# Routing lists of 128 slots instead of 96, and the scatter's list moved from VectorE to ScalarE, in an encoder block with 64 experts

## What is computed

```python
def moe_ffn(x, router_w, router_bias, w_gate, w_up, w_down, sh_gate, sh_up, sh_down):
    scores = sigmoid(xf @ router_w); sel = scores + router_bias
    ...                                   # 4 of 8 groups, then the best 8 of 64 experts
    def expert_block(args):
        tok, e = args
        xb = x_pad[tok]
        hb = jax.nn.silu(xb @ w_gate[e]) * (xb @ w_up[e])
        return hb @ w_down[e]
    ...                                   # each row weighted, then summed into its token
    routed = jax.ops.segment_sum(yb, row_tok, num_segments=n_tok + 1)[:n_tok]
```

## Time and profile before

| | us |
|---|---|
| median of 3 runs (lowest, highest) | 1180.86 (1178.73, 1181.45) |
| the profiled execution | 1178.36 |
| its span | 1176.6 |
| PE busy | 1117.5 (95%) |
| DVE busy | 846.3 (72%) |
| ACT busy | 682.7 (58%) |
| POOL busy | 310.5 (26%) |

### The profile page before, as it was taken

One profiled execution on the slowest core, in us unless ns is written; L12 is line 12 of the kernel. 1 busy time (PEld: TensorE's weight loads), 2 busy tenths in 40 slices (PEclk: granted clock), 3 DMA queues, 4 the chain that ended last, 5 costly groups with the idle time before them and its releaser, 6 DMA issues.

```text
span 1176.6 us, 15711 instructions
## 1 busy us (share of the span) xinstructions
PE 1117.5 (95%) x5390; PEld 840.3 (71%) x5390; DVE 846.3 (72%) x1034; ACT 682.7 (58%) x689; POOL 310.5 (26%) x179
## 2 busy tenths in 40 slices
PE   4999999999999889999999999999999999999796
PEld 3878777768878566777777776777777777676475
DVE  6544436452445586999999988988989988887376
ACT  3332224451223324888888877877878877777354
POOL 1000000000002532444444433432434434231421
PEclk9999999998999899999999999999999999999899
DMA  8522313013345356999999999999999999998721
GB/s 312 179 72 72 99 45 108 1 36 143 108 144 195 138 186 233 346 365 374 369 373 368 369 359 364 366 369 360 353 361 367 368 365 354 364 360 263 257 101 54
DMA packets 68475, 294.78 MB, mean 251 GB/s; under 512 B 11216, under 2 KB 14288, under 8 KB 43600
## 3 DMA queue, kind: packets, MB, share of 16 engines
q1 hardware_dynamic: 52944, 256.43, 57.7%
q0 software_dynamic: 14912, 35.68, 12.3%
q10 hardware_dynamic: 576, 2.10, 0.4%
HBM read 275.29 MB, written 35.65 MB: 264 GB/s over the span
## 4 chain that ended last, share of the span: by engine, by line
PE 36%; DMA 17%; DVE 6%; ACT 3%; issue 3%; ACTq 0%; DVEq 0%; SPq 0%
DMA gu_raw<-in_moe_w_up 11%; PE ps L400 10%; PE ps L402 10%; PE ps L401 9%; DMA gu_raw<-in_moe_w_gate 5%; DVE w_lo L1674 3%; ACT w_hi L1566 3%; PE ps L1475 3%; PE ps L1929 1%; PE ps L1215 1%; PE ps L1499 1%; DVE w_lo L384 1%; PE ps L1466 1%; DVE grp L1283 0%; PE ps L1910 0%
## 5 line engine op out<-in xcount | busy, mean ns | idle before, releaser
L1674 DVE TENSOR_TENSOR w_lo<-gu_raw,w_hi 128x2048 fp32r<-128x2048 f32 x126 | 288.6, 2291 | 52.0 <-ACT w_hi L1566 50.7
L1566 ACT ACTIVATE w_hi<-gu_raw 128x2048 fp32r<-128x2048 f32 x128 | 242.3, 1913 | 53.0 <-DMA gu_raw<-in_moe_w_up 40.7
L400 PE MATMUL ps<-w_hi,xgT_hi 128*96 128x512 f32 x512 | 205.9, 402 | 5.9 <-issue 3.4
L402 PE MATMUL ps<-w_hi,xgT_lo 128*96 128x512 f32 x512 | 203.0, 397 | 0.0
L1777 POOL DMA_INDIRECT xg<-h_rows,get_idx x64 | 149.2, 2331 | 203.5 <-DVE get_idx L1662 171.8
L401 PE MATMUL ps<-w_lo,xgT_hi 128*96 128x512 f32 x512 | 201.6, 394 | 0.0
L400 PE MATMUL ps<-w_hi,act_hi 128*128 128x512 f32 x384 | 155.9, 406 | 5.9 <-PEq L496 2.8
L402 PE MATMUL ps<-w_hi,act_lo 128*128 128x512 f32 x384 | 151.3, 394 | 0.0
L401 PE MATMUL ps<-w_lo,act_hi 128*128 128x512 f32 x384 | 151.1, 393 | 0.0
L1679 DVE TENSOR_TENSOR dn_lo<-dn_raw,dn_hi 128x2048 fp32r<-128x2048 f32 x64 | 146.1, 2282 | 5.7 <-ACT dn_hi L1572 5.3
L1572 ACT ACTIVATE dn_hi<-dn_raw 128x2048 fp32r<-128x2048 f32 x64 | 122.2, 1910 | 12.6 <-issue 8.5
(11 more groups left out here) (203 smaller groups left out, 1722.5 us busy)
## 6 DMA issues: line engine op xcount, KB each, us to landing
gu_raw<-in_moe_w_gate SPq DMA_DIRECT2D x64, 1024.0 KB
gu_raw<-in_moe_w_up SPq DMA_DIRECT2D x64, 1024.0 KB
dn_raw<-in_moe_w_down SPq DMA_DIRECT2D x64, 1024.0 KB
raw<-in_w_in SPq DMA_DIRECT2D x18, 1024.0 KB, 5.1
h_rows<-x_rows SPq DMA_DIRECT2D x8, 512.0 KB, 5.0
raw<-in_w_out SPq DMA_DIRECT2D x4, 1024.0 KB, 5.6
ple_raw<-in_ple_w_gate SPq DMA_DIRECT2D x4, 1024.0 KB, 9.8
x_rows<-in_x SPq DMA_DIRECT2D x4, 512.0 KB, 10.3
```

The lines of the kernel that those rows point to most:

```text
L400: nc.tensor.matmul(out, x_hi, w_hi, start=first, stop=False)
L402: return nc.tensor.matmul(out, x_lo, w_hi, start=False, stop=last)
L1566: nc.scalar.activation(m.w_hi[:, 2 * x.b + half], m.gu_raw[:, 2 * x.b + half], ACT.Copy).then_inc(gu_hi, 1)
L1674: nc.vector.tensor_tensor(m.w_lo[:, 2 * x.b + half], m.gu_raw[:, 2 * x.b + half], m.w_hi[:, 2 * x.b + half].bitcast(F32), ALU.subtract).th ...
```

## The change

The list length goes from 96 to 128. The constant `slots` gets another arrangement: written in bits, partition p = 64h + 32u + 4g + v (h and u one bit, g three, v two) holds slot 32v + 16u + 8h + g. `put_idx` gets four buffers. `put_list(x)` leaves DVE; ACT now does it as the last thing of its step, after `scale_y(x-1)`, with an Identity and a bias from a new constant `far`, and waits for the scatter of x-4 where DVE waited for that of x-2. Two tiles move in memory.

```diff
-SLOTS = 96
+SLOTS = 128
...
-        self.put_idx = [at(f"put_idx{i}", [P, 1], U32, 180.75 + i * 0.0625) for i in range(2)]
+        self.put_idx = [at(f"put_idx{i}", [P, 1], U32, 180.75 + i * 0.0625) for i in range(4)]
...
-        self.hT_lo = at("hT_lo", [P, 2, 2 * cap], F32R, 181)
+        self.hT_lo = at("hT_lo", [P, 2, 2 * cap], F32R, 110)
-        self.onehot = at("onehot", [P, 2, NT, cap], BF16, 182.5)
+        self.onehot = at("onehot", [P, 2, NT, cap], BF16, 181)
...
-    nc.gpsimd.iota(m.slots[:, 0:rounds * cap].rearrange("p (r q j) -> p r q j", r=rounds, q=QUEUES),
-                   pattern=[[cap, rounds], [1, QUEUES], [QUEUES, cap // QUEUES]], base=0, channel_multiplier=0,
-                   allow_small_or_imprecise_dtypes=True)
+    parts = m.slots[:, 0:rounds * cap].rearrange("p (r h u g v) -> p r h u g v", r=rounds, h=2, u=2, g=8)
+    for u in range(2):
+        nc.gpsimd.iota(parts[:, :, :, u], pattern=[[cap, rounds], [8, 2], [1, 8], [32, 4]], base=16 * u,
+                       channel_multiplier=0, allow_small_or_imprecise_dtypes=True)
...
+            def put_list(x, at=99):
+
+                if at not in (0, 2):
+                    act.wait_ge(put[x.b], 16 * (x.turn2 - 2 + ZEROS[x.b]))
+                act.wait_ge(found, x.it + 1 + LEAD)
+                nc.scalar.activation(m.put_idx[x.q][0:CAP],
+                                     m.found[0:CAP, bass.ds(x.e, 1), 0:1].rearrange("p o c -> p (o c)"),
+                                     ACT.Identity, bias=m.far[0:CAP]).then_inc(put_ready, 1)
...
                     if at != 0:
                         scale_y(x.next(-1))
+                    put_list(x, at if first else 99)
...
-            def put_list(x):
-                dve.wait_ge(put[x.b], 16 * (x.turn2 - 1 + ZEROS[x.b]))
-                nc.vector.tensor_scalar(m.put_idx[x.b][0:CAP],
-                                        m.found[0:CAP, bass.ds(x.e, 1), 0:1].rearrange("p o c -> p (o c)"),
-                                        FAR, None, ALU.add).then_inc(put_ready, 1)
...
-                                             out_offset=bass.IndirectOffsetOnAxis(ap=m.put_idx[x.b][0:CAP], axis=0),
+                                             out_offset=bass.IndirectOffsetOnAxis(ap=m.put_idx[x.q][0:CAP], axis=0),
```

More of the change, by code:

```diff
@@ L32 @@
 ROUTED_SCALE = 2.5
-SLOTS = 96
+SLOTS = 128
 FAR = 4096.0
-QUEUES = 16
 HC = 2048
@@ L105, in __init__ @@
         self.peak_i = at("peak_i", [P, 1], I32, 206)
+        self.far = at("far", [P, 1], F32, 206.25)
         self.sh_down = at("sh_down", [P, HC], F32, 0)
@@ L164, in set_constants @@
     nc.gpsimd.memset(m.eps[:], LN_EPS).then_inc(base_set, 1)
-    pool.wait_ge(base_set, 7)
+    nc.gpsimd.memset(m.far[:], FAR).then_inc(base_set, 1)
+    pool.wait_ge(base_set, 8)
     for eye in (m.ident, m.ident_bf):
@@ L765, in _ @@
         def _(act):
-            act.wait_ge(base_set, 7)
+            act.wait_ge(base_set, 8)
             nc.scalar.activation(m.peak[:], m.eps[:], ACT.Sqrt)
@@ L1725, in step @@
                     split_down(x)
-                    if at != -1:
-                        put_list(x)
                 all_experts(dve, r, step)
                 split_hT(Expert(r, QUADS - 1, 3))
-                put_list(Expert(r, QUADS - 1, 3))
             dve.sem_inc(found, LEAD)
```

## The result

| | us |
|---|---|
| before, median of 9 runs (lowest, highest) | 1181.84 (1178.73, 1186.15) |
| after, median of 9 runs (lowest, highest) | 1176.16 (1173.85, 1178.32) |
| ratio, 95% interval | 0.9949, 0.9931 to 0.9967 |
| profiled execution, before and after | 1178.36, 1175.55 |
| its span, before and after | 1176.6, 1173.8 |

The changed kernel is 0.5% faster. The forecast was 1183.0, a little slower. The time that came out is that of rival A, 1176.9, and of rival D, 1177; which of the two mechanisms it was, the profile and the experiments have to tell.

A forecast was written before the change was run, and what follows sets the result against it. Transfers were taken to hold late experts (10.20 us each), a loop over PE, ACT and DVE the early ones. Early loss 0.8, start 0.5 and small packets 0.9 gave +2.2 us on 1178.36, carried to the median 1183.0; range 1172 to 1193.

The forecast's parts named there:

- rival A: Experts' transfers: lists over all 128 partitions make gathers and scatters cheaper, 9.0 us an expert; 1176.9 us; chance 0.22.
- rival D: Experts: faster products and shorter DVE queue count, additions lie in idle time; 4.5 us faster, 1177; chance 0.10.
- What bounds the kernel before: Experts: transfers set the late pace, 10.20 us each; early a loop of 9.70, measured 9.77, with transfers close behind.
- The loop: PE, ACT and DVE passing two experts: 19.39 us, plus 0.67 added, less 0.15, gives 19.91, 9.96 an expert.
- the transfers: Experts: same rows and weights moved, so late ones stay at 10.20 us; early ones lose 4.4, 3.6 given back.
- the forecast case: Whole kernel: the prediction's own outcome, 1183.0 us, from 1179 to 1187 by its bounds; chance 0.45.
- rows 12: Profile window read as a gather: 0.33 us a row, weights beside it at 25.6 GB/s an engine.
- signs put down for A: Experts: a gathered row at 0.16 us, or a DMA share clearly below 1.0, would show rival A.
- What the change removes: DVE between dn_lo and hT_lo: one 96x1 instruction and its wait go, worth nothing; four lists free nobody else.
- Small packets: Transfers: places without a row add 4096 packets of 9 ns, 2.3 us of the 16 engines, 0.9 counted.
- Rival B: Experts' transfers: the new arrangement loads the 16 engines unevenly; 11 us slower, 1194; chance 0.12.
- Rival C: Experts: the loop is longer than summed, 10.35 us instead of 9.96; 1191 taken; chance 0.11.

The follow-up runs named there:

- e1: Kernel before with only the scatter's list moved to ACT, last in the step, four buffers, lists still 96: 1178.83 us, ratio 0.9993.
- e5: e1 with all its transfers but 12 of 24 gate_up products and lighter work on ACT and DVE, lists of 96: 1175.38 us, ratio 0.9957 to before.
- e11: e10's code with lists of 96 in the arrangement of before: 1178.64 us, ratio 0.9998 to before.
- e6: Changed kernel with all its transfers and the same light work as e5, lists of 128: 1131.76 us, ratio 0.9592 to before.
- e7: e5 with every place of the scatter's lists out of range, so scatters move no rows: 1089.82 us, ratio 0.9232 to before.
- e9: e2 with four buffers for the scatter's list instead of two, list still on DVE: 1171.69 us, ratio 0.9937 to before.
- e2: Kernel before with lists of 128 in the new arrangement, scatter's list still on DVE with two buffers: 1192.28 us, ratio 1.0094.
- e3: Changed kernel with the old arrangement of slots (partition 8q + j holds slot 16j + q): 1242.6 us, ratio 1.0516 to before.
- e12: e6 with the old arrangement of slots (partition 8q + j holds slot 16j + q): 1227.14 us, ratio 1.0394 to before.
- e4: Changed kernel with the scatter's list made on ACT ahead of silu instead of behind the scaling of rows: 1173.49 us, ratio 0.9922 to before.
- e10: e4 with the gather's list moved to ACT too, lists of 128: 1160.8 us, ratio 0.9838 to before.

## Why the prediction was wrong

**What bounds the kernel before** was read rightly. Early experts 9.77 and late 10.20, the loop close below: e1, e5 and e11 confirm that with lists of 96 the transfers hold the pace (10.05, 10.11, 10.01 us), whatever is taken off the loop.

**The loop** was summed rightly. Predicted were 19.91 us for two experts; 19.95 were measured in one step. (The lower bound, given as 9.87 for one expert, is 9.84 by its own terms: 19.39 + 0.43 - 0.15, halved.) Its terms, from the groups of the whole span after (mean ns behind the busy us):

```profile
L1690 DVE TENSOR_TENSOR xgT_lo<-ps,xgT_hi 128x1024 fp32r<-128x1024 f32 x64 | 77.9, 1218 | 3.9 <-ACT xgT_hi L1578 3.9
...
L1661 DVE TENSOR_TENSOR onehot<-slots,slot_of 128x512 bf16<-128x512 f32 x64 | 44.0, 691 | 1.7
...
L1587 ACT ACTIVATE hT_hi<-ps 128x256 fp32r<-128x256 f32 x64 | 23.9, 373 | 0.0
...
L1594 ACT ACTIVATE put_idx<-found,far 128x1 uint32 x52 | 14.7, 282 | 0.0
```

xgT_lo +0.27 (0.27 predicted), one_hot +0.135 (0.14), hT_hi +0.06 (0.07), the list 0.28 long and `w_hi` 1.46 us behind the scaling instead of 1.22, so +0.24 for list and hT_hi together (0.26). PE's products follow each other a little faster; 21 of them in the kernel after:

```profile
1082.37 0.39 PE L402 MATMUL ps<-w_hi,xgT_hi 128*128 128x512 f32 x1
...
1087.13 0.39 PE L402 MATMUL ps<-dn_hi,hT_hi 128*128 128x512 f32 x1
```

That is 4.76 us, 0.2267 each (0.2276 predicted, 0.2317 with 96). The weight loads did get longer. The groups of PEld in 480 to 1062 us, before and after:

```profile
L400 PEld LDWEIGHTS ps<-w_hi,xgT_hi 128*96 128x96 f32 x463 | 74.9, 162 | 34.8 <-issue 3.8 <-DVE xgT_lo L1684 2.2
...
L402 PEld LDWEIGHTS ps<-w_hi,xgT_hi 128*128 128x128 f32 x466 | 87.4, 187 | 31.5 <-DVE xgT_lo L1690 9.4 <-issue 5.1
```

162 to 187 ns, 25 more, and in a row of products all of it is hidden behind the product ahead. The rule of the Trainium skill ("TensorE: Matmul & The Clock Gate", LDWEIGHTS), an estimated 27 ns, agrees on the load and has no say in the pace. PE's part of the loop fell by 0.04 us where 0.15 were counted: the second product of gate_up starts 0.34 us behind the first instead of 0.28, that of down 0.32 instead of 0.28, which takes back most of the gain; why wasn't looked into. Scaling to gate_up grew by 0.60 where 0.67 were counted, so the sum comes out well in part because two misses go opposite ways.

**The step that failed is the transfers.** The prediction said: the rows moved are the same and the weights too, so the late stretch stays at 10.20. Transfers alone fell from 10.11 to 9.36 us an expert (e5, e6), and the late stretch went to the loop's pace, 9.98: 8.3 us won where 0 were counted. The early stretch lost 6.8 us where 0.8 were counted (4.4, less 3.6 that the late one was to give back). This was rival A, with its mechanism, its sum (the loop holds all 60 experts, early ones longer, late ones shorter) and nearly its time, but with a chance of 0.22. One of the signs put down for A came true as well: in the trace's record of single packets a gathered row takes 0.159 us in the kernel after (median), where it took 0.194. That 1176.16 lies within the stated 1172 to 1193 is no credit to the forecast case, which ended at 1179.

It was put aside because of a **mislabelled row**. The captions and the prediction took the earlier trace rows for a scatter and the earlier trace rows for a gather, because in the timeline of POOL in the kernel before (first three rows below) a scatter starts at 549.83 and a gather at 554.26, just ahead of each window. But the rows of a transfer move some 4 to 6 us after its instruction starts on POOL. That shows in e7 (last two rows), where only gathers move rows:

```profile
544.66 2.74 POOL L1777 DMA_INDIRECT xg<-h_rows,get_idx  x1 [2.96 <-DVE get_idx L1662]
549.83 1.46 POOL L1789 DMA_INDIRECT residual_rows<-y,put_idx  x1 [2.44 <-ACT y L1591]
554.26 2.74 POOL L1777 DMA_INDIRECT xg<-h_rows,get_idx  x1 [2.98 <-DVE get_idx L1662]
...
526.69 1.46 POOL L1792 DMA_INDIRECT residual_rows<-y,put_idx  x1 [5.24 <-ACT put_idx L1594]
530.00 0.98 POOL L1780 DMA_INDIRECT xg<-h_rows,get_idx  x1 [1.86 <-DVE get_idx L1674]
```

The gather that starts at 530.00 moves its rows in 534.1 to 537.5, and the scatter of 526.69 passes, empty, in 531.3 to 533.6. So the earlier trace rows is the gather issued at 544.66 and the earlier trace rows the scatter issued at 549.83. At the end of the kernel before, where no gather is left, the window 1069 to 1073 shows the scatter's price:

```profile
q0 software_dynamic: 112, 0.30, 38.4%
```

73 rows in 0.384 x 16 x 4 = 24.6 us are 0.33 us a row, the figure that the prediction gave to the gather. The record of single packets leaves no doubt: none of the 65 rows of 4 KB in the earlier trace rows takes over 0.24 us, and the 63 in the earlier trace rows and the 73 here all take 0.33. With the labels the right way round, says that the weights fall from 26.6 to 21.3 GB/s an engine beside a *gather*, a writer of SBUF over 96 partitions, and the earlier trace rows that they keep 25.6 beside a *scatter*, which writes HBM. The sentence against rival A ("the slow neighbour is the scatter, which writes HBM") would have become the strongest row for it. Its other sentence, that rows 12 agree with rival A's rule in the slow row alone, falls too: that slow row is a scatter's, and what fits the rival is the slowed weights of the earlier trace rows. Rival A's price of a gather was wrong in its parts for the same reason: 0.7 us for faster rows (0.12 measured) and 0.5 for the neighbours (0.39).

**What the change removes** was half right. Moving the list gains nothing at 96 (e1) and nothing at 128 (e9). But "four lists instead of two free nobody else" was wrong: at 128 the wait for the scatter of x-2 becomes real, and two buffers would cost 1.6% (e2, e9). The row of before (DVE idle 0.62 us there) couldn't show a wait that the change itself was going to make.

**Small packets.** 4096 more passed on q0 (19008 instead of 14912). e6 has them all and is 43.6 us faster than e5; they vanish behind the rest.

**Rival B** (uneven engines) didn't happen, because the new arrangement does fit the engines; e3 and e12 show its mechanism and its size where an arrangement doesn't: 1.1 us an expert in the whole kernel and 1.6 in the transfers alone, 66 us in e3's median against the kernel after, six times the 11 us that the prediction gave it. **Rival C** fell: the loop is 9.98. **Rival D** fell too: the early experts got longer by 0.30, so the additions do lie on the loop. That its time, 1177, came out is chance.

## What to carry to other kernels

Before a window of the DMA view is given to a transfer, find a stretch where only that kind moves (the end, where no gather is left, was on record): a software transfer's bytes move several us behind its instruction, and a window around the issue shows its neighbour. Where two bounds lie within 5%, run each alone; a pair of kernels with the transfers kept and the arithmetic thinned out (e5, e6) settled here what no share could. Count buffers again when a transfer grows, since a wait that costs nothing today becomes real once the landing takes longer than a step.

## What the runs showed of the hardware

- A gather over 96 partitions costs its neighbours more than itself: 0.39 us an expert by slower weights (22.4 instead of 26.0 GB/s an engine) against 0.12 by its own slower rows (0.19 and 0.16 us a row of 4 KB).
- A row of 4 KB that is added into HBM takes an engine 0.33 us, twice a gathered one, and hardly slows its neighbours: the weights keep 25.6 GB/s an engine, and the 1.34 us an expert that the scattered rows cost (e5 to e7) are little more than their own 64 x 0.33 / 16 = 1.32.
- Which partition a slot lies on is worth 1.6 us an expert with the same bytes where the transfers run alone (e6 against e12, 8% of the time), and 1.1 in the full kernel (after against e3, 6%).
- A DMA share of 1.01 doesn't mean that the transfers are the bound. After, e4, e9 and e10 all show 1.01 at paces from 10.01 down to 9.79 us, while e6 needs 9.36. In the trace's record of single packets the weights' packets of 8 KB beside a gather have a median of 309 ns in after as in e6, but one in a hundred takes over 1200 ns in after, against 324 in e6. What makes these few long when the loads are issued late wasn't tried and stays open. The mean share also hides that engines rest: fewer than 16 packets are under way in 12% of 480 to 940 us in after, against 3% in the kernel before.
- The head of the kernel varies: expert 1 starts between 458 and 464 us in before, after, e1 to e4 and e9 to e11, though little of the change lies ahead of it. For a change in the experts the pace over 60 of them is the steadier measure.
